# Layer 0's transposes of query and key heads, placed behind other gate groups

## The reference, cut to what matters

```
lf, lgq, lgk, lgv, lwq, lwk, lwv, lgate = split_proj(h  @ w_in)     # latent tokens
cf, cgq, cgk, cgv, cwq, cwk, cwv, cgate = split_proj(hc @ w_in)     # context tokens
q_g = apply_rope(rms_norm(heads(lgq, 8), q_norm_g), cos, sin)       # likewise k_g, q_w, k_w
o_g = global_attention(q_g, k_g, v, kc_g, vc_g); o_w = window_attention(...)
g   = sigmoid(gate_cols)                                            # 3 x 1024 gates a token
m   = g0*(fourier_mix(lf) @ w_f) + g1*(o_g @ w_g) + g2*(o_w @ w_w);  y = m @ w_out
```

## Time and profile before

| what | value |
|---|---|
| median of 3 runs | 2349.38 us (2349.33 to 2354.11) |
| the profiled execution's own time | 2353.92 us |
| its span | 2352.1 us |
| PE busy (matmuls) | 2005.3 us, 85% |
| PE weight loads | 1107.7 us, 47% |
| DVE busy | 622.8 us, 26% |
| ACT busy | 434.8 us, 18% |
| DMA | 576.35 MB, 245 GB/s in the mean |
| TensorE clock granted, mean | 0.961 |

### The profile page before, as it was taken

How to read it: one execution, slowest core, us unless ns; L and a number is a source line. 1 busy time by engine, 2 the same in 40 slices (tenths; PEclk the granted TensorE clock), 3 DMA queues, 4 the chain that set the end, 5 groups by cost and what they waited for, 6 DMA issues and landing times.

```text
span 2352.1 us, 31618 instructions
## 1 busy us (share of the span) xinstructions
PE 2005.3 (85%) x13636; PEld 1107.7 (47%) x13636; DVE 622.8 (26%) x1480; ACT 434.8 (18%) x1095; POOL 21.5 (1%) x42
## 2 busy tenths in 40 slices
PE   6998999998988888889999775666776699989997
PEld 4444554456433444334768431233332247564765
DVE  2021550135112222223361401201111235323542
ACT  2122621113111111002251110100000212222222
POOL 2000000000000000000000000000000000000000
PEclk9999999998999999999999888899998899999999
DMA  8554225415999999994313389999999733233320
GB/s 283 179 179 143 73 90 178 162 63 188 402 423 422 422 422 417 421 418 145 133 37 143 139 337 423 423 416 412 417 416 419 309 108 108 97 118 107 108 81 18
DMA packets 133912, 576.35 MB, mean 245 GB/s; under 512 B 7448, under 2 KB 16128, under 8 KB 92816
## 3 DMA queue, kind: packets, MB, share of 16 engines
q1 hardware_dynamic: 130752, 567.31, 60.9%
q0 software_dynamic: 2512, 6.84, 1.0%
q10 hardware_dynamic: 512, 0.19, 0.0%
HBM read 573.26 MB, written 1.05 MB: 244 GB/s over the span
## 4 chain that ended last, share of the span: by engine, by line
PE 52%; DMA 22%; issue 8%; PEld 7%; DVE 4%; ACT 3%; PEldq 3%; SPq 0%; ACTq 0%; DVEq 0%
DMA ring<-w_up_e 16%; PE ps L753 7%; PE ps L1198 5%; PE ps L742 5%; PE ps L1111 4%; PE ps L939 4%; PE ps L1206 3%; PEld ps L1142 3%; PEldq L687 3%; PE ps L769 2%; PE ps L1339 2%; DMA ring<-w_down_e 2%; DMA ring<-w_xkv 2%; PE ps L667 1%; DMA ring<-w_in 1%
## 5 line engine op out<-in xcount | busy, mean ns | idle before, releaser
L1111 PE MATMUL ps<-ring,reg_bc 128*32 128x512 f32 x3072 | 395.5, 651 | 150.1 <-DMA ring<-w_up_e 140.0
L1111 PEld LDWEIGHTS ps<-ring,reg_bc 128*32 128x32 f32 x3072 | 94.4, 115 | 427.0 <-DMA ring<-w_up_e 227.4
L753 PE MATMUL ps<-reg_a,ring 128*128 128x512 f32 (+1 forms) x768 | 256.5, 491 | 6.8 <-issue 4.2
L753 PEld LDWEIGHTS ps<-reg_a,ring 128*128 128x128 f32 x768 | 144.1, 191 | 106.0 <-issue 91.9
L1198 PE MATMUL ps<-ring,reg_a 128*128 128x512 f32 (+2 forms) x448 | 147.9, 486 | 8.0 <-issue 6.0
L2276 DVE TENSOR_TENSOR xall<-xall,ps 128x512 f32<-128x512 f32 x48 | 32.8, 687 | 451.6 <-PE ps L1083 451.6
L1703 ACT ACTIVATE reg_bc<-ps 128x512 f32<-128x512 f32 x48 | 28.7, 597 | 583.4 <-PE ps L1111 583.4
L2319 DVE TENSOR_TENSOR reg_a<-ps,reg_e 32x256 f32<-32x256 f32 x192 | 80.7, 421 | 196.3 <-PE ps L1142 193.9
L1142 PE MATMUL ps<-ring,reg_bc 128*32 128x256 f32 x2048 | 117.1, 380 | 15.6 <-issue 14.2
L742 PE MATMUL ps<-ring,reg_a 128*128 128x512 f32 (+1 forms) x288 | 112.8, 546 | 1.9 <-issue 1.5
L1198 PEld LDWEIGHTS ps<-ring,reg_a 128*128 128x128 f32 x448 | 76.1, 196 | 74.0 <-issue 70.9
(11 more groups left out here) (340 smaller groups left out, 2151.2 us busy)
## 6 DMA issues: line engine op xcount, KB each, us to landing
ring<-w_gate_e SPq DMA_DIRECT2D x128, 1024.0 KB, 11.2
ring<-w_up_e SPq DMA_DIRECT2D x128, 1024.0 KB, 14.3
ring<-w_down_e SPq DMA_DIRECT2D x64, 2048.0 KB, 14.9
ring<-w_in SPq DMA_DIRECT2D x34, 2048.0 KB, 8.4
ring<-w_ada SPq DMA_DIRECT2D x24, 2048.0 KB, 8.0
ring<-w_out SPq DMA_DIRECT2D x8, 2048.0 KB, 8.2
ring<-w_xkv SPq DMA_DIRECT2D x8, 1024.0 KB, 15.2
ring<-w_br_global SPq DMA_DIRECT2D x4, 1024.0 KB, 6.4
```

The source lines that it names most:

```text
L753: mm = pe.matmul(ps[j][:, 0:n], w[:, k, j * P:(j + 1) * P], HT[:, k, 0:n], start=(k == 0), stop=(k == KC - 1))
L1111: mm = pe.matmul(ps[s][32 * j:32 * j + 32, :], XGT[:, s, 2 * q + k, e * CAP:(e + 1) * CAP], w[:, j // 2, k, (j % 2) * COL:(j % 2 + 1) * CO ...
```

## The change

A table `heads_at(l, b, j)` now says which pairs of heads are transposed behind gate group (b, j). PE's and ACT's streams both take it, so ACT copies the pairs in the places that answer to PE's. In layer 0 nothing follows groups (1, 0) and (1, 1); pairs 0 and 1 follow (1, 2) and (1, 3); pairs 2 and 3 both follow (2, 0), pairs 4 and 5 both follow (2, 1); pairs 6 and 7 stay behind (2, 2) and (2, 3). Layer 1 keeps its places. The number of instructions, their operands, the slabs and the banks are the same.

```diff
@@ -401,6 +401,12 @@
+    def heads_at(l, b, j):
+
+        if l:
+            return (2 * j, 2 * j + 1) if b == 2 else ()
+        return {(1, 2): (0,), (1, 3): (1,), (2, 0): (2, 3), (2, 1): (4, 5), (2, 2): (6,), (2, 3): (7,)}.get((b, j), ())
@@ -871,11 +877,8 @@   (PE)
                         else:
                             ada_turn(ada)
-                        if b:
-                            turn_heads(0, 4 * (b - 1) + j)
-                    elif b == 2:
-                        turn_heads(1, 2 * j)
-                        turn_heads(1, 2 * j + 1)
+                    for m in heads_at(l, b, j):
+                        turn_heads(l, m)
                 last_release(pe)
@@ -1588,11 +1591,8 @@   (ACT)
                         else:
                             ada_column(ada)
-                        if b:
-                            heads_in(0, 4 * (b - 1) + j)
-                    elif b == 2:
-                        heads_in(1, 2 * j)
-                        heads_in(1, 2 * j + 1)
+                    for m in heads_at(l, b, j):
+                        heads_in(l, m)
```

## The result

| | before | after |
|---|---|---|
| median of the paired runs | 2355.07 us (8 runs, 2349.33 to 2359.15) | 2342.57 us (8 runs, 2337.62 to 2345.91) |
| ratio | | 0.9950, 95% interval 0.9936 to 0.9964 |
| profiled execution, its span | 2353.92, 2352.1 us | 2342.03, 2340.2 us |

The change makes the kernel 12.50 us faster by the medians; 12.53 had been worked out. The interval of the ratio leaves 8.5 to 15.1 us, so that the two agree to 0.03 us is luck; that they agree to a few microseconds is not. But the forecast time, 2336.9 us, and its range, up to 2342.5, start from a median of 2349.38 that three runs had given. Eight runs, these three among them, put it at 2355.07. So the difference was right and the level was not: the measured median lies 5.7 us above the forecast and 0.07 us above the range.

A forecast was written before the change was run, and what follows sets the result against it. PE was taken to bound the kernel, with a 10.36 us wait for DVE. 12.84 for wait and half clock plus 0.55, less 0.86 for moved transposes, gave 12.53; 2349.38 - 12.5 = 2336.9 us, range 2332.5 to 2342.5.

The forecast's parts named there:

- The wait and where it goes: Layer 0, PE before pair 0: the 10.36 us wait for DVE's head norms vanishes, with 6.1 us to spare.
- The rebuilt sum: PE's layer 0 stretch from the product at 173.71: ninth group 13.39 us earlier, less 0.86 for moved heads, net 12.53.
- The half clock as a second price, 2.48 us: Behind PE's layer 0 wait: 2.04 us for a group and 0.44 for transposes at half clock, both regained.
- The extra transposes: Pairs 3 and 5 moved behind (2, 0) and (2, 1): 0.43 us each, 0.86 in all, hidden by nothing.
- No wait for a bank: Doubled pairs in layer 0, waiting for ACT's copies: taken as 0, at most 0.80 us per place, 1.6 for both.
- The slab's wait: PE before the ninth gate group: the 0.26 us wait for weights stays; any change in the load is below 0.5.
- What comes later: Everything behind 200 us, experts included, starts 12.5 us earlier with the same distances; the whole gain is counted.
- Rival C: The wait moves to pair 0's new place through slower DVE, or experts' weights take the time back: 2345 to 2352, chance 0.08.
- Rival D: Runs of eight transposes lower attention's clock: up to 61 us added, 2398; chance 0.04 with anything like it.
- so from the median: 2349.38 - 12.5: Last step for the whole kernel: the gain taken from the median of the runs, not the profiled 2353.92, giving 2336.9 us.
- The clock later: Later low-clock stretches may lengthen or shorten when shifted: two half-clock groups of 2.04 us, 4.1 us in either direction.

The follow-up runs named there:

- Experiment 3: Changed kernel with pair 0 behind the sixth gate group and pairs 3 and 4 both behind (2, 0); 2346.30 us against 2353.22 before, ratio 0.9963.
- experiment 1: Kernel before, with 10 unneeded matmuls put ahead of pair 0's wait in layer 0; 2352.27 us against 2353.22, ratio 0.9991.
- experiment 4: Changed kernel with all eight pairs of layer 0 behind the four groups of b = 2, two at a time; 2343.49 us, ratio 0.9951 to before.
- experiment 2: Kernel before, with DVE's rotation of the heads left out in layer 0; 2341.56 us, 11.66 less, ratio 0.9954.

## Why the prediction was right and wrong

- *The wait and where it goes*: right. It was to vanish with 6.1 us to spare; DVE ended at 186.48 and the product at 192.01, 5.5 us later; pair 0 came at 192.32 (forecast 192.2). Experiment 3 puts pair 0 one group earlier and gets the remainder as a wait of 2.90.
- *The rebuilt sum*: right. Sixth group 175.94 (forecast 176.04), seventh 182.99 (183.09), eighth 192.79 (192.74), ninth 200.62 (200.57). Attention started 12.46 us earlier (12.53), 12.35 counted from the product at 173.60. The missing 0.2 is mostly the idle time of 0.31 before pair 0, which the neighbour's 2.69 (product, one pair, group; here 2.84) didn't have.
- *The half clock as a second price, 2.48 us*: right, measured by itself as 2.44 in experiment 1.
- *The extra transposes*: 0.92 and 0.88 us for eight, forecast 0.87. No wait for a bank, as taken; experiment 4 doubles the key pairs in layer 0 as well and finds none.
- *The slab's wait*: 0.26 before and after, though the bracket now says issue.
- *What comes later*: right as far as the runs can tell. The shift is 12.27 us at the first expert slab and 11.9 at the last gate-and-up matmul in the pair of traces shown, with some 4 us of scatter between executions at both; experiment 2 gains 11.66 us in time (6.1 to 15.5) from 10.8 at attention.
- *Rival C*: DVE's chain took 17.19 us with PE at work beside it, 17.17 before. None of the wait moved to another place.
- *Rival D*: the clock stood at 1.00 from 186 to 237 us, the stretch with the two runs of eight transposes, and kept 1.00 for the 66 us of attention. The Trainium skill ("TensorE: Matmul & The Clock Gate", Part 4) says that transposes don't count as work for the clock the way matmuls do, and by this the change could have cost clock; no run here shows that it did.
- *The step that failed* is the last of the sum, "so from the median: 2349.38 - 12.5". The term that was mis-sized is the level: 2349.38 stood on three runs, two of them at 2349.3 and one at 2354.11, beside a profiled execution of 2353.92. Two of these four lay at 2354, and I took them for the upper edge of the scatter; they were its middle. The eight runs beside the changed kernel put it at 2355.07, 5.69 us higher, and that is the whole of the 5.7 us by which the forecast was off. 65 runs give 2354.11, and 2354.11 - 12.53 = 2341.6 is within 1.1 us of every median of the changed kernel (2342.57, 2342.67, 2342.00). *The clock later*, where 4.1 us were allowed for dips, had named what probably makes the scatter, but as something that the shift might change. It needs no shift: executions of one and the same kernel differ by 9.2 us in the tail alone (507.4 to 516.6). The range had no term for the level of before.

What stays open: what makes an execution take one pattern of dips and not another, and how the part ahead of the tail contributes. There the last gate-and-up matmul started at 1829.3, 1826.8 and 1825.1 us in three profiles of the changed kernel.

## What to carry to other kernels

A wait on the engine that sets the end costs its length and can cost a slow stretch behind it (here 2.44 us behind 10.36); look in the windows for the clock behind it. Rebuild the stretch from the durations of undisturbed neighbours, place by place: here every start came out to 0.12 us and the whole to 0.2. The stream order is the first thing to look at when an engine waits with independent work right behind the wait: moving the waiting piece past it cost next to nothing here, and the two places tried behind the end of the awaited chain were equally good. Forecast the difference, and give the level a scatter of its own: three runs and a profile that disagree by 0.2% are a warning that the median isn't known to better than that.

## What the hardware showed unexpectedly

The same wait of 2.58 us of TensorE was followed by 7.14 us of work in one execution and 10.19 in another of the same kernel, at a granted clock of 1.00 and 0.50. The tail had a few lengths (506 to 507, 510 to 511, 517 us) over eleven traces with the same code there. A wait of 10.36 us in the first block was followed by 0.50 in the one trace of it, one of 2.90 and one of 2.04 us weren't, in one trace each. And in a stage that goes at the pace of the weights, raising the clock from 0.85 to 0.95 moved neither the rate of the weights (385 and 386 GB/s) nor the time.
